# A mixture-of-experts decoder step: four weight units of the last job fetched before the expert loop

## The chip, the cores and the metric

The kernel runs on one core of a Trainium2 chip. The metric is the device time of one execution in microseconds (us); lower is better. The engines are named as in the profile: PE (TensorE, matrix products; PEld is its weight load), DVE (VectorE), ACT (ScalarE), POOL (GpSimd) and SP (SyncE, which here only starts transfers). Sixteen DMA engines move the data; SP, ACT and POOL each have a queue of their own into them.

## The reference

One decoder layer on 512 prompt rows and 8 sample rows of width 1024. A mixer (pooling, dilated attention, gated convolution) and an output projection come first, then a layer norm, then a mixture of experts:

```python
logits = einsum('md,de->me', xt, router_w) + router_b      # 520 rows, 32 experts
top_v, top_i = top_k(logits, 4);  gates = softmax(top_v)
hh = xblk @ e_w_in[e] + e_b_in[e]                           # 1024 -> 2048
gate, up = split(hh, 2);  gate = min(gate, 7);  up = clip(up, -7, 7)
act = gate * sigmoid(1.702 * gate) * (up + 1)
y += gate_weight * (act @ e_w_out[e] + e_b_out[e])          # 1024 -> 1024
x = layer_norm(alpha * x + y)
```

Everything is in 32-bit floats. An expert has 8 MB of input weights and 4 MB of output weights, and all 32 experts are used, so the expert weights are some 400 MB.

## The kernel before

There are two program blocks, one after the other, with a barrier of all engines between them.

**The front** (`first_block`) does the mixer, the projection, the first layer norm, the router, and the lists of rows for each expert. It keeps the attention's mix in `mix` (`[P, 8, 520]`) and queries, keys, values and bias rows in `qkv` (`[P, 6*520+2048]`). While it ends, SP fetches the first expert's twelve units into `ring` (L270): three at L565 and later, four after the last attention product, five after the last output projection (`wo3`). POOL splits the output biases into `drow` (L650, L653), which reads `qkv`, and then scatters the row lists to memory (L629). When all lists are there (`listed`), SP reads back six pieces of them (L585, L587) and ACT two (L816). At the same time DVE works out the job table (L1441 to L1502): which expert each job has, and how many groups of 32 rows. So the job order is known only at the end of the front.

**The expert loop** (`moe_block`) runs over jobs, 32 here, one for each expert. The order is by row count through the table `ORDER`; the last job has the expert with the fewest rows. A job has 1 to 5 groups of 32 rows. Its weights are twelve **units** of 1 MB: 8 input units (`ring[0..7]`) and 4 output units (`ring[8..11]`). The ring holds one job's worth, so a unit's slot is loaded anew as soon as PE has used it. The steps of PE for job u are:

- `up`: a bias product (L1747), then for each of 8 input units a wait for it, and the products of each group (L1753; eight PE records for a unit and group);
- `down` of the job before: bias (L1772, L1778), then for each of 4 output units a wait and the products (L1767; sixteen records for a unit and group).

SP, in its loop (around L1621), waits for `up_done` of each input unit of job u and loads that of job u+1, then waits for `down_done` of each output unit of job u-1 and loads that of job u. All weights go through its one queue, in this order: in(u+1) 0 to 7, out(u) 0 to 3, in(u+2) 0 to 7, and so on. DVE turns PE's results into the next operand (`xgT`, `hid`), ACT does the sigmoid and scales the results (L1821), POOL gathers rows (L1667) and adds results into memory (L1676). After the last job the sums are read into `fin` (`[P, 5, 1024]`, a buffer of its own) and the second layer norm ends the program.

PE's groups are a nest of branches, written so that a job with few groups jumps over the code of the others in each unit:

```python
def each_group(groups, f, j=0):
    if j + 1 < JG:
        with pe.If(groups > j + 1):
            each_group(groups, f, j + 1)
    return f(j)
```

Of the kernel before, what the change touches and what calls it, by code (L numbers as in the profile page):

```python
# [29 lines left out]
P = 128  # L30
D = 1024
KT = D // P
SEQ = 512
NS = 8
R = SEQ + NS
HALF = R // 2
NT = SEQ // P
# [18 lines left out]
GS = 32  # L56
# [9 lines left out]
NWORD = -(-(MAXJ + 1) // 3)  # L66
AHEAD = 6
UNITS = 12
LAST_TILES = (4, 0, 1, 2, 3)
PAD0 = R + 4  # L70
ORDER = (0, 30, 10, 9, 15, 11, 22, 1, 25, 21, 24, 7, 18, 5, 17, 14, 23, 2, 28, 19, 4, 16, 12, 26, 8, 20, 3, 27, 6, 29, 13, 31)
# [162 lines left out]
def layer(nc, xT, x_prompt, x_sample, pool_prefix, conv_prefix, state_pool, state_conv, cache_k, cache_v,  # L234
          w_in, pool_w, chan, w_o, ln1_g, ln1_b, router_w, router_b, e_in, e_brow, e_out, e_bout,
          ln2_g, ln2_b, consts, lists0, pbias,
          y_prompt, y_sample, p_pool, p_conv, p_k, p_v, s_pool, s_conv, s_k, s_v):
    x1_dram = nc.dram_tensor("x1_rows", [R, D], F32).ap()
    acc_dram = nc.dram_tensor("acc_rows", [R, D], F32).ap()
    q_dram = nc.dram_tensor("sample_queries", [NS, ATTW], F32).ap()  # L240
    lists_dram = nc.dram_tensor("list_rows", [GS, NE * MAXQ, 2], F32).ap()

    with ExitStack() as outer:
        def keep(name, shape, dt=F32):
            return outer.enter_context(nc.sbuf_tensor(name, shape, dt))

        def sem(name):
            return outer.enter_context(nc.semaphore(name))


        ring = keep("ring", [P, UNITS, 2048])
        cst = keep("cst", [P, NCONST])
        lists = keep("lists", [P, NE * MAXQ, 2])
        brow = keep("brow", [P, NQ, 2, QC], BF16)
        drow = keep("drow", [P, D], BF16)
        jobs = keep("jobs", [1, 6, NJT], I32)
        count = keep("job_count", [1, 1], I32)

        def C(name, rows=P):
            lo, hi = CONST[name]  # L260
            return cst[0:rows, lo:hi]

        unit_in = [sem(f"unit_in{u}") for u in range(UNITS)]
        lists_in = sem("lists_in")
        more_lists_in = sem("more_lists_in")

        def load_unit(eng, e, j):

            src = e_in[bass.ds(e, 1), j] if j < KT else e_out[bass.ds(e, 1), j - KT]
            eng.dma_start(ring[:, j], src.rearrange("o p n -> p (o n)")).then_inc(unit_in[j], 16)  # L270

        first_block(nc, locals())
        moe_block(nc, locals())
# [3 lines left out]
def first_block(nc, o):  # L277

    xT, x_prompt, x_sample, w_in, w_o, cache_k, cache_v, state_pool, state_conv = (
        o[k] for k in "xT x_prompt x_sample w_in w_o cache_k cache_v state_pool state_conv".split())  # L280
    ring, lists, lists_in, more_lists_in, jobs, count, brow, drow, C, load_unit = (
        o[k] for k in "ring lists lists_in more_lists_in jobs count brow drow C load_unit".split())
    x1_dram, acc_dram, lists_dram, q_dram = o["x1_dram"], o["acc_dram"], o["lists_dram"], o["q_dram"]


# [29 lines left out]
    with ExitStack() as ctx:  # L315
        def sb(name, shape, dt=F32):
            return ctx.enter_context(nc.sbuf_tensor(name, shape, dt))

        def bsem(name):
            return ctx.enter_context(nc.semaphore(name))  # L320
# [2 lines left out]
        late = xt[:, :, :].rearrange("p k r -> p (k r)")  # L323
        l1g, l1b = late[:, 0:D], late[:, D:2 * D]
        x1t = late[:, 2 * D:4 * D].rearrange("p (u k r) -> p u k r", u=2, k=KT)
        mix = sb("mix", [P, KT, R])
        scr = mix[:, 2:4, :]
        scr2 = mix[:, 4:6, :]
        prod = mix[:, 2:4, :].rearrange("p a r -> p (a r)")[:, 0:2 * ATTW].rearrange("p (t f) -> p t f", t=2)
        up = sb("up", [P, 2, PBUF + R])  # L330
        qkv = sb("qkv", [P, 6 * R + 2 * FF])
        qT = qkv[:, 0:3 * R].rearrange("p (i r) -> p i r", i=3)
        kT = qkv[:, 3 * R:6 * R].rearrange("p (i r) -> p i r", i=3)
        v = qkv[:, 6 * R:6 * R + (NT + 1) * ATTW].rearrange("p (i f) -> p i f", f=ATTW)
# [121 lines left out]
        counted = bsem("counted")  # L456
        ranks_read = bsem("ranks_read")
        split = bsem("bias_split_steps")
        brow_ready = bsem("brow_ready")
        placed_in_lists = bsem("placed_in_lists")  # L460
        listed = bsem("listed")
# [30 lines left out]
        def _(sp):  # L492
# [87 lines left out]
            sp.wait_ge(stored, 16 * (NT + 1 + 4))  # L580
            sp.wait_ge(copied, 48)
            sp.wait_ge(k_stored[1], 32)
            sp.wait_ge(listed, 16 * TOPK * (NT + 1))
            for c in (0, 2):
                sp.dma_start(lists[c * GS:(c + 1) * GS, 0:NE * JG], lists_dram[:, 0:NE * JG]).then_inc(lists_in, 16)  # L585
            for c in range(NQ):
                sp.dma_start(lists[c * GS:(c + 1) * GS, NE * JG:], lists_dram[:, NE * JG:]).then_inc(more_lists_in, 16)  # L587

        @block.gpsimd
        def _(gp):  # L590
# [67 lines left out]
                keep_high_out(part * NE, (part + 1) * NE)  # L658
            take_off_out(2 * NE, 3 * NE)
            keep_high_out(2 * NE, 3 * NE)  # L660
            for i in range(NT):
                list_rows(i, i + 2)

        @block.scalar
        def _(a):
# [146 lines left out]
                x1_store(i, i + 2)  # L812
                top_exps(i, i + 2)
            a.wait_ge(listed, 16 * TOPK * (NT + 1))
            for c in (1, 3):
                a.dma_start(lists[c * GS:(c + 1) * GS, 0:NE * JG], lists_dram[:, 0:NE * JG]).then_inc(lists_in, 16)  # L816
            a.wait_ge(x1_sent, 32 * (NT + 1))

        @block.tensor
# [708 lines left out]

def moe_block(nc, o):

    ring, lists, lists_in, more_lists_in, brow, drow, jobs, count, C, sem, load_unit, unit_in = (
        o[k] for k in "ring lists lists_in more_lists_in brow drow jobs count C sem load_unit unit_in".split())
    x1_dram, acc_dram = o["x1_dram"], o["acc_dram"]
    x1_quarters = x1_dram.rearrange("r (c n) -> (r c) n", n=QC)
    acc_quarters = acc_dram.rearrange("r (c n) -> (r c) n", n=QC)
# [1 line left out]
    with ExitStack() as ctx:  # L1537
# [16 lines left out]
        gate4 = sb("gate4", [P, AHEAD, JG])  # L1554
        l2g = sb("l2g", [P, D])
        l2b = sb("l2b", [P, D])
        fin = sb("fin", [P, NT + 1, D])
        zeros = sb("zeros", [P, 1], BF16)
        bn2 = sb("bn2", [P, 2, 2, 6])
        mv2 = sb("mv2", [P, NT + 1, 5])  # L1560
# [49 lines left out]
        def _(sp):  # L1610
# [10 lines left out]
            with sp.Fori(1, MAXJ) as u:  # L1621
                with sp.If(u + 1 < last):
                    e = expert_of(u + 1)
                    for k in range(KT):
                        sp.wait_ge(up_done, KT * u + k + 1)
                        load_unit(sp, e, k)
                with sp.Else():
                    sp.nop()
                with sp.If(u < last):
                    e = expert_of(u)  # L1630
                    for q in range(FT // 2):
                        sp.wait_ge(down_done, FT // 2 * u + q + 1)
                        load_unit(sp, e, KT + q)
                with sp.Else():
                    sp.nop()
# [96 lines left out]
        def _(pe):  # L1732
# [10 lines left out]
            def up(groups, step):  # L1743

                def bias(j):
                    for c in range(NQ):
                        nc.tensor.matmul(pu[quarter(c), j], chosen[:, :], brow[:, c],  # L1747
                                         start=True, stop=False, skip_group_check=True)

                def unit(k, j):  # L1750
                    w = ring[:, k].rearrange("p (a n) -> p a n", a=2)
                    for c in range(NQ):
                        mm = nc.tensor.matmul(pu[quarter(c), j], xgT[:, j, k], w[:, :, c * QC:(c + 1) * QC],  # L1753
                                              start=False, stop=k == KT - 1, skip_group_check=True)
                    return mm
                each_group(groups, bias)
                for k in range(KT):
                    pe.wait_ge(unit_in[k], 16 * step)
                    each_group(groups, lambda j: unit(k, j)).then_inc(up_done, 1)

# [261 lines left out]
```

## Time and profile before

| | |
|---|---|
| median of 3 runs | 1390.07 us (1389.95 to 1390.19) |
| the profiled execution's own time | 1392.93 us |
| its span, first to last instruction | 1390.8 us |
| mean granted TensorE clock | 0.948 of full |
| PE busy | 1210.8 us (87%) |
| DVE busy | 509.2 us (37%) |
| moved by DMA | 463.13 MB |
| share of the DMA engines, SP's queue | 77.8% |

The span is some 2 us shorter than the execution's own time, and that execution took 2.86 us more than the median of the runs. Busy time of PE is from modelled ends of pipelined matmuls. In the rows, "x8" is a count of instructions, and the brackets give idle time before them with what ended it.

### The profile page before, as it was taken

What the parts mean: (1) busy time and instruction counts of PE and PEld (TensorE: products, weight loads), DVE (VectorE), ACT (ScalarE), POOL (GpSimd) and SP (SyncE); (2) the same over time, 40 slices, a digit from 0 to 9 for tenths busy, and PEclk for the clock granted to TensorE, in tenths of its full rate; (3) what the DMA queues carried; (4) which work ended last, traced back from release to release, by engine and by line L of the source; (5) the groups of instructions that cost most, each with busy time, mean ns of one, the idle gap of its engine ahead of it and who ended that gap; (6) DMA issues with size and microseconds to landing.
All of it is one profiled execution on the core that took longest, in us unless ns stands there. A gap on an engine that the chain in (4) does not pass through costs nothing.

```text
span 1390.8 us, 33184 instructions
## 1 busy us (share of the span) xinstructions
PE 1210.8 (87%) x12380; PEld 539.8 (39%) x12381; DVE 509.2 (37%) x825; ACT 177.6 (13%) x351; POOL 314.5 (23%) x263
## 2 busy tenths in 40 slices
PE   6998989883789999999979998998998989996880
PEld 5886434361233333344333433362342323432230
DVE  1997624275422222224231332132222231414226
ACT  0013222220010000001000010010000010101103
POOL 7000112624121232013212132124121212130113
PEclk9999999975899999999999999999999999998975
DMA  9601840281999999999999999999999999999973
GB/s 342 193 3 61 263 163 3 95 311 53 410 415 417 409 406 400 416 409 394 414 416 407 414 404 414 392 414 397 416 409 405 408 416 407 381 401 419 408 292 125
DMA packets 86538, 463.13 MB, mean 333 GB/s; under 512 B 13508, under 2 KB 29609, under 8 KB 36205
## 3 DMA queue, kind: packets, MB, share of 16 engines
q1 hardware_dynamic: 67915, 438.55, 77.8%
q0 software_dynamic: 16528, 17.88, 5.9%
q10 hardware_dynamic: 2066, 6.32, 1.2%
q8 instruction: 17, 0.28, 0.1%
q14 instruction: 12, 0.10, 0.0%
HBM read 448.29 MB, written 19.48 MB: 336 GB/s over the span
## 4 chain that ended last, share of the span: by engine, by line
PE 51%; DMA 19%; issue 3%; DVE 2%; SPq 1%; ACT 0%; DVEq 0%; ACTq 0%; POOLq 0%
PE pu L1753 32%; PE rest L1767 17%; DMA ring<-in_e_in 12%; DMA ring<-in_e_out 6%; PE pu L1747 1%; PE rest L1778 1%; SPq L270 1%; DVE fin L1954 0%; DVE bn L1936 0%; DVE mv L1947 0%; DMA acc_rows<-y,idx 0%; PE rest L1772 0%; DMA fin<-acc_rows 0%; DVE xgT L1875 0%; ACT y L1821 0%
## 5 line engine op out<-in xcount | busy, mean ns | idle before, releaser
L1753 PE MATMUL pu<-ring,xgT 128*32 128x512 f32 x5248 | 592.1, 604 | 36.6 <-DMA ring<-in_e_in 34.9
L1753 PEld LDWEIGHTS pu<-ring,xgT 128*32 128x32 f32 x5248 | 164.2, 111 | 445.8 <-issue 443.2
L1767 PE MATMUL rest<-ring,hid 128*32 128x256 f32 x5248 | 299.6, 384 | 18.4 <-DMA ring<-in_e_out 12.5
L1676 POOL DMA_INDIRECT acc_rows<-y,idx x82 | 130.4, 1591 | 763.2 <-ACT y L1821 734.3
L1905 DVE TENSOR_SCALAR gg<-pu 128x1280 f32<-128x1280 f32 x32 | 47.7, 1492 | 613.1 <-PE pu L1753 604.6
L1767 PEld LDWEIGHTS rest<-ring,hid 128*32 128x32 f32 x5248 | 177.4, 111 | 130.9 <-issue 35.0
L1813 ACT ACTIVATE ss<-gg 128x1280 f32<-128x1280 f32 x32 | 40.7, 1273 | 670.6 <-DVE gg L1905 670.6
L836 PE MATMUL pair<-xt,ring 128*128 128x260 f32 x448 | 101.1, 389 | 12.3 <-DMA ring<-in_w_in 12.3
L1667 POOL DMA_INDIRECT xq<-x_rows,idx x82 | 86.1, 1050 | 57.2 <-issue 44.8
L836 PEld LDWEIGHTS pair<-xt,ring 128*128 128x128 f32 x448 | 86.6, 194 | 25.7 <-DMA ring<-in_w_in 12.0
L1821 ACT ACTIVATE y<-rest,gate 128x256 f32 x160 | 61.9, 479 | 252.6 <-PE rest L1767 252.6
L1162 DVE SCALAR_TENSOR_TENSOR conv<-conv,chan_sb 128x512 f32<-128x512 f32 x90 | 70.2, 779 | 3.1
L1747 PE MATMUL pu<-brow,chosen 128*32 128x512 bf16 x328 | 25.1, 403 | 42.9 <-issue 30.1
L1875 DVE STREAM_TRANSPOSE xgT<-xq 128x1280 f32<-128x1280 f32 x33 | 49.7, 1505 | 0.0
L1922 DVE STREAM_TRANSPOSE hid<-uu 128x1280 f32<-128x1280 f32 x32 | 48.2, 1505 | 0.0
L1917 DVE TENSOR_TENSOR uu<-uu,ss 128x1280 f32<-128x1280 f32 x32 | 47.7, 1492 | 1.1
L1915 DVE SCALAR_TENSOR_TENSOR uu<-uu,gg 128x1280 f32<-128x1280 f32 x32 | 47.5, 1484 | 0.0
L1907 DVE TENSOR_SCALAR uu<-pu 128x1280 f32<-128x1280 f32 x32 | 47.4, 1481 | 0.0
L641 POOL TENSOR_SCALAR ring<-ring,negm 128x128 f32<-128x128 f32 (+3 forms) x24 | 26.9, 1125 | 87.6 <-DVE negm L1404 87.5
L1920 DVE CAST chosen_down<-cst 128x32 bf16 x32 | 5.8, 182 | 107.2 <-PE rest L1767 104.1
L968 PE MATMUL pair<-ring,mix 128*128 128x512 f32 x80 | 35.8, 594 | 0.0
L1747 PEld LDWEIGHTS pu<-brow,chosen 128*32 128x32 bf16 x328 | 6.5, 97 | 61.9 <-issue 59.6
(264 smaller groups left out, 613.4 us busy)
## 6 DMA issues: line engine op xcount, KB each, us to landing
ring<-in_e_in SPq DMA_DIRECT2D x256, 1024.0 KB
ring<-in_e_out SPq DMA_DIRECT2D x128, 1024.0 KB
ring<-in_w_in SPq DMA_DIRECT2D x3, 1536.0 KB, 24.0
ring<-in_w_in SPq DMA_DIRECT2D x6, 512.0 KB, 12.4
xt<-in_xT SPq DMA_DIRECT2D x2, 1040.0 KB, 11.0
ring<-in_w_o SPq DMA_DIRECT2D x1, 2048.0 KB, 12.0
conv<-in_x_prompt SPq DMA_DIRECT2D x1, 2048.0 KB, 13.7
x_rows<-conv ACTq DMA_DIRECT2D x4, 512.0 KB
```

The source lines that it names most:

```text
L836: mm = nc.tensor.matmul(b[:, h, 0:HALF], wtile[:, tiles_of(lo, lo + P).start, k], xt[:, k, h * HALF:(h + 1) * HALF], start=k == 0, stop=k ...
L1162: ch.mark(V.scalar_tensor_tensor(cy[:, i, 0:SEQ], u[:, i, t:t + SEQ], taps[:, i, t:t + 1], cy[:, i, 0:SEQ], ALU.mult, ALU.add))
L1667: nc.gpsimd.indirect_dma_start(out=xq[:, u % 2, j], out_offset=None, in_=x1_quarters, in_offset=bass.IndirectOffsetOnAxis(ap=idx4[:, u % A ...
L1676: nc.gpsimd.indirect_dma_start(out=acc_quarters, out_offset=bass.IndirectOffsetOnAxis(ap=idx4[:, u % AHEAD, j:j + 1], axis=0), in_=y[:, u ...
L1753: mm = nc.tensor.matmul(pu[quarter(c), j], xgT[:, j, k], w[:, :, c * QC:(c + 1) * QC], start=False, stop=k == KT - 1, skip_group_check=True)
L1767: mm = nc.tensor.matmul(py[quarter(c), j], hid[:, j, 2 * q + f], w[:, f, c * QC:(c + 1) * QC], start=False, stop=q == FT // 2 - 1 and f == ...
L1821: ins = nc.scalar.activation(y[:, bass.ds(u % 2, 1), j].rearrange("p o n -> p (o n)"), py[:, j], ACT.Copy, scale=ring4[:, bass.ds((u % AHE ...
L1875: V.transpose(xgT[:, :, :, :].rearrange("p j k s -> p (j k s)"), xq[:, half].rearrange("p j n -> p (j n)")).then_inc(turned, 1)
L1905: V.tensor_scalar(gg[:, :, :], pu[:, :, 0], SW_LIMIT, None, ALU.min).then_inc(g_ready, 1)
L1915: at.do(V.scalar_tensor_tensor(uu[:, :, :], uu[:, :, :], 1.0, gg[:, :, :], ALU.add, ALU.mult))
L1917: V.tensor_tensor(uu[:, :, :], uu[:, :, :], ss[:, :, :], ALU.mult).then_inc(h_ready, 1)
L1922: V.transpose(hid[:, :, :, :].rearrange("p j f s -> p (j f s)"), uu[:, :, :].rearrange("p j n -> p (j n)")).then_inc(hid_ready, 1)
```

## The change

A constant `KEPT = 4` and one more buffer, `shared`, that lives through both blocks. In the front, `mix` and `qkv` are now views of it; at the end, `fin` is. Between the two uses its first four units' worth, `last_up`, holds input units 0 to 3 of expert index 31, fetched in the front. SP does this right after expert 0's last five units, once POOL has ended the split of the output biases (`drow_ready`). SP no longer waits for the lists; ACT issues all eight list loads. In the loop SP leaves out units 0 to 3 for the last job, and PE reads them from `last_up` there.

```diff
+        shared = keep("shared", [P, KT * R + 6 * R + 2 * FF])
+        last_up = shared[:, 0:KEPT * 2048].rearrange("p (k n) -> p k n", n=2048)
...
+        def load_last_up(eng, k):
+            eng.dma_start(last_up[:, k], e_in[NE - 1, k]).then_inc(last_up_in, 16)
...
-        mix = sb("mix", [P, KT, R])
+        mix = shared[:, 0:KT * R].rearrange("p (k r) -> p k r", r=R)
...
-        qkv = sb("qkv", [P, 6 * R + 2 * FF])
+        qkv = shared[:, KT * R:]
...
             sp.wait_ge(k_stored[1], 32)
-            sp.wait_ge(listed, 16 * TOPK * (NT + 1))
-            for c in (0, 2):
-                sp.dma_start(lists[c * GS:(c + 1) * GS, 0:NE * JG], lists_dram[:, 0:NE * JG]).then_inc(lists_in, 16)
-            for c in range(NQ):
-                sp.dma_start(lists[c * GS:(c + 1) * GS, NE * JG:], lists_dram[:, NE * JG:]).then_inc(more_lists_in, 16)
+            sp.wait_ge(drow_ready, 1)
+            for k in range(KEPT):
+                load_last_up(sp, k)
...
             keep_high_out(2 * NE, 3 * NE)
+            gp.sem_inc(drow_ready, 1)
...
             a.wait_ge(listed, 16 * TOPK * (NT + 1))
-            for c in (1, 3):
+            for c in range(NQ):
                 a.dma_start(lists[c * GS:(c + 1) * GS, 0:NE * JG], lists_dram[:, 0:NE * JG]).then_inc(lists_in, 16)
+            for c in range(NQ):
+                a.dma_start(lists[c * GS:(c + 1) * GS, NE * JG:], lists_dram[:, NE * JG:]).then_inc(more_lists_in, 16)
...
-        fin = sb("fin", [P, NT + 1, D])
+        fin = shared[:, 0:(NT + 1) * D].rearrange("p (i n) -> p i n", n=D)
...
                     e = expert_of(u + 1)
-                    for k in range(KT):
+                    with sp.If(u + 2 < last):
+                        for k in range(KEPT):
+                            sp.wait_ge(up_done, KT * u + k + 1)
+                            load_unit(sp, e, k)
+                    with sp.Else():
+                        sp.nop()
+                    for k in range(KEPT, KT):
                         sp.wait_ge(up_done, KT * u + k + 1)
                         load_unit(sp, e, k)
...
-                for k in range(KT):
+                with pe.If(step < last):
+                    for k in range(KEPT):
+                        pe.wait_ge(unit_in[k], 16 * step)
+                        each_group(groups, lambda j: unit(k, j)).then_inc(up_done, 1)
+                with pe.Else():
+                    pe.wait_ge(last_up_in, 16 * KEPT)
+                    for k in range(KEPT):
+                        each_group(groups, lambda j: unit(k, j, last_up)).then_inc(up_done, 1)
+                for k in range(KEPT, KT):
                     pe.wait_ge(unit_in[k], 16 * step)
                     each_group(groups, lambda j: unit(k, j)).then_inc(up_done, 1)
```

## Rows read from the trace of the kernel before

**Rows 1.** The page's chain that ended last, shares of the span by line.
```profile
PE pu L1753 32%; PE rest L1767 17%; DMA ring<-in_e_in 12%; DMA ring<-in_e_out 6%; PE pu L1747 1%; PE rest L1778 1%; SPq L270 1%; DVE fin L1954 0%; DVE bn L1936 0%; DVE mv L1947 0%; DMA acc_rows<-y,idx 0%; PE rest L1772 0%; DMA fin<-acc_rows 0%; DVE xgT L1875 0%; ACT y L1821 0%
```

**Rows 2.** Windows 385:655 and 655:1335: busy time of each engine, granted clock, DMA share, GB/s.
```profile
385.00:655.00 270.00, 261.57 (x3222) 104.22 (x3222) 74.05 (x82) 27.60 (x53) 63.52 (x48) 1.00 1.03 408
655.00:1335.00 680.00, 612.12 (x7412) 232.89 (x7407) 190.20 (x210) 67.37 (x126) 136.71 (x103) 0.98 1.02 407
```

**Rows 3.** Waits of PE, 385 to 655: us in total, times, longest.
```profile
PE pu L1747 <- issue: 8.3, 9, 1.7
```

**Rows 4.** Waits of PE, 655 to 1336.
```profile
PE pu L1753 <- DMA ring<-in_e_in: 34.6, 36, 1.9
PE rest L1767 <- DMA ring<-in_e_out: 12.5, 14, 2.1
```

**Rows 5.** Timeline of PE at the end: start us, us, what, count, idle before.
```profile
1313.43 1.07 PE L1767 MATMUL rest<-ring,hid 128*32 128x256 f32 x16 [1.41 <-DMA ring<-in_e_out]
...
1315.93 1.07 PE L1753 MATMUL pu<-ring,xgT 128*32 128x512 f32 x8 [0.23 <-issue]
1318.40 1.07 PE L1753 MATMUL pu<-ring,xgT 128*32 128x512 f32 x8 [1.41 <-DMA ring<-in_e_in]
...
1333.88 1.94 PE L1753 MATMUL pu<-ring,xgT 128*32 128x512 f32 x8 [0.54 <-DMA ring<-in_e_in]
...
1336.63 11.21 PE L1767 MATMUL rest<-ring,hid 128*32 128x256 f32 x192
...
1351.29 5.61 PE L1767 MATMUL rest<-ring,hid 128*32 128x256 f32 x64
```

**Rows 6.** Timeline of SP's queue at the end: in(31), then out(30) and out(31).
```profile
1290.32 18.35 SPq L270 DMA_DIRECT2D ring<-in_e_in  x8
1309.84 38.55 SPq L270 DMA_DIRECT2D ring<-in_e_out  x8
```

**Rows 7.** Windows 1332:1334 and 1336:1338, columns as in rows 2.
```profile
1332.00:1334.00 2.00, 1.46 (x12) 0.12 (x8) 0.00 (x0) 0.00 (x0) 0.00 (x0) 0.50 0.57 242
1336.00:1338.00 2.00, 2.00 (x28) 0.90 (x32) 2.00 (x2) 0.59 (x1) 0.00 (x0) 0.50 0.23 98
```

**Rows 8.** Timeline of POOL in the front: last step of the bias split, last list scatter.
```profile
268.83 1.03 POOL L650 CAST drow<-qkv 32x1024 bf16<-32x1024 f32 x1
...
321.92 0.98 POOL L629 DMA_INDIRECT list_rows<-pairs,spots  x1 [0.30 <-issue]
```

**Rows 9.** Timeline of SP's queue in the front.
```profile
290.62 0.54 SPq L270 DMA_DIRECT2D ring<-in_e_out  x1
...
324.96 1.82 SPq L587 DMA_DIRECT2D lists<-list_rows  x4
```

**Rows 10.** Timeline of ACT in the front: last store of normed rows, list loads.
```profile
308.54 0.45 ACTq L751 DMA_DIRECT2D acc_rows<-conv  x1
...
324.06 0.88 ACTq L816 DMA_DIRECT2D lists<-list_rows  x2
```

**Rows 11.** Timeline of DVE around the barrier.
```profile
329.91 0.19 DVE L1502 SCALAR_TENSOR_TENSOR jobs<-xt 1x52 int32<-1x52 f32 x1
331.07 0.17 DVE L1866 COPY gate<-lists 128x5 f32<-128x5 f32 x1 [0.97 <-PEq L315]
...
335.43 0.16 DVE L1866 COPY gate<-lists 128x5 f32 x1
```

**Rows 12.** Windows 290:312 and 312:322 of the front, columns as in rows 2.
```profile
290.00:312.00 22.00, 17.83 (x93) 16.36 (x92) 15.26 (x59) 7.07 (x15) 7.94 (x8) 0.58 1.00 383
312.00:322.00 10.00, 2.34 (x21) 1.81 (x20) 7.74 (x43) 0.39 (x2) 6.94 (x8) 0.50 0.03 5
```

**Rows 13.** Timeline of PE: start and products of a five-group job, then a one-group job.
```profile
540.88 1.26 PE L1747 MATMUL pu<-brow,chosen 128*32 128x512 bf16 x20 [0.49 <-issue]
541.96 34.51 PE L1753 MATMUL pu<-ring,xgT 128*32 128x512 f32 x320
...
907.97 7.08 PE L1753 MATMUL pu<-ring,xgT 128*32 128x512 f32 x64
```

More of the change, by code:

```diff
@@ L68 @@
 UNITS = 12
+KEPT = 4
 LAST_TILES = (4, 0, 1, 2, 3)
@@ L263, in layer @@
         unit_in = [sem(f"unit_in{u}") for u in range(UNITS)]
+        last_up_in = sem("last_up_in")
         lists_in = sem("lists_in")
@@ L280, in first_block @@
         o[k] for k in "xT x_prompt x_sample w_in w_o cache_k cache_v state_pool state_conv".split())
-    ring, lists, lists_in, more_lists_in, jobs, count, brow, drow, C, load_unit = (
-        o[k] for k in "ring lists lists_in more_lists_in jobs count brow drow C load_unit".split())
+    ring, shared, lists, lists_in, more_lists_in, jobs, count, brow, drow, C, load_unit, load_last_up = (
+        o[k] for k in "ring shared lists lists_in more_lists_in jobs count brow drow C load_unit load_last_up".split())
     x1_dram, acc_dram, lists_dram, q_dram = o["x1_dram"], o["acc_dram"], o["lists_dram"], o["q_dram"]
@@ L458, in first_block @@
         split = bsem("bias_split_steps")
+        drow_ready = bsem("drow_ready")
         brow_ready = bsem("brow_ready")
@@ L1529, in moe_block @@
 def moe_block(nc, o):
-    ring, lists, lists_in, more_lists_in, brow, drow, jobs, count, C, sem, load_unit, unit_in = (
-        o[k] for k in "ring lists lists_in more_lists_in brow drow jobs count C sem load_unit unit_in".split())
+    ring, shared, last_up, lists, lists_in, more_lists_in, brow, drow, jobs, count, C, sem, load_unit, unit_in, last_up_in = (
+        o[k] for k in ("ring shared last_up lists lists_in more_lists_in brow drow jobs count C sem load_unit unit_in "
+                       "last_up_in").split())
     x1_dram, acc_dram = o["x1_dram"], o["acc_dram"]
@@ L1748, in bias, with unit @@
                                          start=True, stop=False, skip_group_check=True)
-                def unit(k, j):
-                    w = ring[:, k].rearrange("p (a n) -> p a n", a=2)
+                def unit(k, j, of=ring):
+                    w = of[:, k].rearrange("p (a n) -> p a n", a=2)
                     for c in range(NQ):
```

## The prediction

> **What bounds the kernel now.** I read the chain that ended last, then the windows, then PE's waits, and last the timelines of PE and of SP's queue at the end. In the chain the reader is to see that PE's two products and the transfers of the two kinds of weights share the span, 49% to 18% [rows 1]. That alone does not say which of the two sets the end. The windows do: from 385 to 1335 us the DMA engines are busy throughout (share 1.03 and 1.02, at 408 and 407 GB/s), while PE is busy 261.57 of 270 and 612.12 of 680 us [rows 2]. Up to 655 PE waits for no transfer at all, only some 0.9 us at the start of each of nine steps [rows 3]. After 655 it waits for weights 50 times, 47.1 us in all [rows 4]. So the stream of weights has no gap and sets the time; PE works close behind it and absorbs what it can in those 50 waits. A byte that leaves this stream should shorten the span, if PE does not become the limit where it leaves, and if the byte's new place is free.
>
> **What the change takes out at the end.** The last job has one group, so PE does a unit of it in 1.07 us at full clock, and it stands waiting for the next: its units 1 and 7 start at 1318.40 and 1333.88 [rows 5], which is 15.48 / 6 = 2.58 us a unit. The queue order behind that is in(31) 0 to 7, out(30) 0 to 3, then out(31) 0 to 3 [rows 6]. The change leaves out in(31) 0 to 3, so everything behind in the queue comes 4 x 2.58 = 10.3 us earlier. The queue does not run dry through this: out(29) 3 lands just before 1313.43 [rows 5], and in(31) 4 to 7 are issued when up(30) frees their slots, by 1308.3 (the end of 18.35 us from 1290.32, less the last issue) [rows 6].
>
> Then PE's side, step by step, because the whole 10.3 us counts only if PE follows:
>
> - up(31) starts at 1315.9 as before. Units 0 to 3 lie ready: 4 x 1.07 = 4.3 us, to 1320.2. Unit 4 is in by then; unit 7 comes at 1333.88 - 10.3 = 1323.6 and its product ends at 1324.7.
> - down(30), three groups, began at 1336.63 and took 11.21 us [rows 5]. If out(30) follows in(31) at the same pace, its units are usable at 1326.2, 1328.8, 1331.3 and 1333.9. PE's 11.21 us began at half clock (granted 0.50 until 1338 [rows 7]); at full clock throughout I estimate 10.5, or 2.6 us a unit, the pace of the transfers. So it goes from 1326.2 to 1336.7. Before, it ended at 1347.84. That is 11.1 us.
> - down(31) waits, from the end of down(30), for DVE to turn `hid` and for ACT to empty the sums; that took 1351.29 - 1347.84 = 3.45 us and does not change. So it starts at 1340.2. out(31) is issued as the slots come free, after each unit of down(30), as now. It moves with down(30), and its 5.61 us too.
> - What follows, 1356.9 to 1390.8 = 33.9 us (last scatter, reading the sums, layer norm, stores), is the same work; `fin` has a new address only.
>
> The extra 0.8 us beyond 10.3 is clock and wait. The granted clock was 0.50 at the last units of up(31) [rows 7], each of which took 1.94 instead of 1.07 us [rows 5]; before the fall PE had worked 1.07 of each 2.5 us. With four units at hand PE is busy nearly all the time from 1315.9, and I expect full clock there.
>
> One thing in the rows has to be settled for this sum. The DMA share falls to 0.57 at 1332 to 1334 and to 0.23 at 1336 to 1338 [rows 7], yet down(30) shows no wait. Most engines thus have finished out(30) by 1334, and a few, 0.23 x 16 = 4 or fewer, work on. A unit counts as in only when its last engine is done, so the 2.58 us pace is that of the slowest engines, and I let out(30) land at that pace. If all sixteen were even, out(30) would be in by about 1334 now and 1324 then; down(30) would start right behind up(31), at 1325.2, end at 1335.7, and the gain would be 12.1 us. The Trainium skill ("DMA: Bandwidth & Descriptors", Latency and other measured facts) says that DMA engines 7 and 15 are usually slower than the others in traces; by that rule the first of the two sums, 11.1 us, is the right one, and the window at 1336 agrees in kind, with a share near that of a few engines.
>
> **What it adds in the front.** 4 MB more from SP's queue. SP issues expert 0's last unit at 290.62 [rows 9]; the bias split for which it now waits ended at 269.9 [rows 8], so that wait costs nothing, and nothing is behind it on SP but the barrier. The four issues take about 1.8 us (four list loads took 1.82 [rows 9]). The transfers need 10.3 us. The engines are full from 290 to 312 and nearly idle from 312 to 322 [rows 12], so the traffic ends near 322.5 instead of 312. ACT's last store of normed rows is issued at 308.54 [rows 10] and will land later, but is awaited only after the lists. The lists are what matters: POOL's last scatter is issued at 321.92 to 322.9 [rows 8] and seen as landed at 324.1, when the list loads start [rows 10]. The new traffic has ended about then, on slow engines perhaps 2 us later.
>
> The list loads themselves: ACT issues eight instead of two, 0.44 us each [rows 10], so its last starts 2.6 us later than its second did, at about 327.2, against SP's last now at 326.4 [rows 9]. Nobody needs them yet: DVE writes the job table until 330.1, all engines pass the barrier at 331.0, and DVE reads the first lists at 331.07 and the second part at 335.43 [rows 11]. The slack is some 3 us for ACT to reach the barrier, and 5 us or more for the second part. Bounds: 0 if all lands as said; 3 us if a list scatter is held up behind weights and the barrier moves; below 0 there is nothing, since SP's own list loads were not on the path. I take 0.2.
>
> If the cover of idle engines from 312 to 322 were gone, the fetch would cost its 10.3 us again and the change would be worth nothing but the 0.8.
>
> **What it adds in the loop.** On SP one comparison and a branch a job, before the first load; the queue is far ahead (in(31) unit 0 is issued at 1290.32 and unit 1 used at 1318.40 [rows 5, 6]), so 0. On PE a comparison in each step, and after unit 3 a jump over the new code of the other branch: 4 units x 5 groups x 16 instructions = 320. The trace has no such jump. From below: a one-group job jumps over 64 instructions in each of 8 units, and its 64 products take 7.08 us where the five-group job's pace gives 64 x 34.51 / 320 = 6.90 [rows 13]; that is 0.02 us a jump. From above: the start of a step, with the jump back over the whole body, three waits and several branches, shows 0.49 us [rows 13] and at most 1.7 [rows 3]. By length the new jump is nearer to the first, and I take 0.1 us. Nine steps without a wait for transfers make 0.9 us, behind a stream that has no gap there, and after 655 the 47.1 us of waits take the rest: 0 on the path. With 0.5 us a step the nine steps make 4.5 us, of which I would still expect most hidden.
>
> **The sum.** 11.1 - 0.2 = 10.9 us. The profiled execution took 1392.93 us, span 1390.8, so the same view of the changed kernel should show a span of 1379.9. The median of the runs was 2.86 us under the profiled execution's time; the same difference in time from the median is 1390.07 - 10.9 = **1379.2 us**.
>
> **Rivals.**
>
> 1. *The jump is dear.* The start of a step can cost 1.5 us or so, and the new jump lands 320 instructions on. If it cost 1.5 us, the nine steps to 655 would make PE 13.5 us late where it has no wait to give back; the ring would fill, the stream would stop, and the net would be at worst 1390.07 - 10.9 + 13.5 = 1392.7, slower. It turns from gain to loss at 10.9 / 9 = 1.2 us a step, later if the ring's stock covers a part. For it: 8.3 us in nine starts [rows 3]. Against it: 0.02 us a jump within units [rows 13]. The Trainium skill ("Runtime: NRT & Kernel Launch", Instruction fetch mechanics) says that a taken branch whose target is outside the window of fetched pages stalls until the page is there, and gives the page as 256 instructions; by that rule each of the 31 steps pays a fetch, and no row here shows its length for such a jump. Half price, 0.5 to 1.2 us, gives 1380 to 1390. Chance: 0.05 for slower, 0.08 for a part of the gain lost.
> 2. *The front slips.* Scatters of the lists wait behind 4 MB of weights, and the barrier moves by 1 to 3 us: 1380.5 to 1382.5. For it: the engines are full until 322 and POOL's last scatter is issued at just that time. Against: POOL issued eight of them beside full engines from 301 on (x8 in 290 to 312 [rows 12]), and each is small. Chance 0.13.
> 3. *The clock falls anyway.* PE's busy share before 1315.9 is low in both kernels. At half clock up(31) takes 8 x 1.94 = 15.5 us to 1331.4, and down(30) ends at 1343: the gain is 5, 1385. Chance 0.05.
> 4. *The fetch replaces nothing.* If SP's skip starved the queue, in(31) 4 would be late; it is issued near 1300, 13 us before out(29) 3 lands, so I give this 0.02, at 1388 to 1391.
>
> The forecast itself has 0.67. From these: faster by over 0.2% (2.8 us, about what a measurement of this kernel can tell from no change) 0.91, within 0.2% 0.04, slower 0.05. The range for 8 in 10 takes in the even-engine sum (1378.0 with nothing lost in front) and the slipped front up to 1383.
>
> **What would show it.** In the profile after: the DMA share in 312 to 322 near 1 instead of 0.03; the barrier still near 331; the first 28 jobs at the same times to within 1 us; up(31) without a wait in its first four units and with full clock; down(30) ending near 1336.7; the DMA share falling below 0.6 near 1322; 33.9 us after PE's last product. If the starts of steps are unchanged but a gap of more than 0.5 us stands inside `up` after unit 3, rival 1 is at work. If the whole loop is shifted by a constant from 331 on, rival 2. If the span falls by less than 8 us with neither, the queue order was not what set the end.

## The result: the changed kernel is slower by 31%

The changed kernel took 1824.3 us (1822.5 to 1827.8, four runs), the kernel before 1390.0 us on the same chip (1387.5 to 1390.2, four runs). The ratio is 1.313, 95% interval 1.311 to 1.315. The profiled execution has a span of 1821.6 us against 1390.8, and a mean granted clock of 0.866 against 0.948. Some executions are longer for no reason in the kernel (1442.4 us of e6, 1447.3 and 1458.4 of e11, 2535.5 of e10 in the experiments below), and the ratios leave them out.

The forecast was 1379.2 us, with a range from 1378.0 to 1383. What the change was meant to do does happen at the end, as e4 and e12 show; but PE's loop has grown by one branch, and that makes each of its 31 full steps 13.9 us longer.

The changed kernel leaves one thing out: it fetches the four units of expert 31 and uses them for whichever expert has the last job. On this input that is expert 12 with 10 rows, while expert 31 has 22 rows and an earlier job (e11's expectation gives both counts). So the first four units of the last job are another expert's, and the results of those 10 rows are not the reference's. The same holds for e4, e6, e7, e8, e10 and e12; e11 and e13 put expert 31 last. The number and size of products and transfers are the same either way, so the times can be compared.

### The profile page after: what moved, and what is told of

Same layout as the page of the kernel before. It is cut to its first block, busy times and chain, and to the rows that moved or that the text cites. A ratio compares the mean times of both kernels' runs of the same rounds, so it can differ in the third digit from the quotient of the medians.

```text
span 1821.6 us, 33355 instructions
## 1 busy us (share of the span) xinstructions
PE 1328.5 (73%) x12380; PEld 549.9 (30%) x12381; DVE 508.6 (28%) x825; ACT 177.5 (10%) x351; POOL 313.1 (17%) x263
## 3 DMA queue, kind: packets, MB, share of 16 engines
q8 instruction: 290, 4.75, 1.1%
## 4 chain that ended last, share of the span: by engine, by line
PE 57%; issue 22%; DVE 1%; DMA 0%; ACT 0%; DVEq 0%; ACTq 0%; POOLq 0%
PE pu L1770 36%; PE rest L1792 18%; PE pu L1764 2%; PE rest L1803 1%; DVE shared L1979 0%; DVE bn L1961 0%; PE rest L1797 0%; DVE mv L1972 0%; DMA acc_rows<-y,idx 0%; DVE xgT L1900 0%; ACT y L1846 0%; DMA shared<-acc_rows 0%; DVE idx L1892 0%; ACT shared L1875 0%; DVE shared L1990 0%
## 5 line engine op out<-in xcount | busy, mean ns | idle before, releaser
L1770 PE MATMUL pu<-ring,xgT 128*32 128x512 f32 x5216 | 650.8, 657 | 115.3 <-issue 115.3
L1792 PE MATMUL rest<-ring,hid 128*32 128x256 f32 x5248 | 337.7, 409 | 96.8 <-issue 96.2
L1770 PEld LDWEIGHTS pu<-ring,xgT 128*32 128x32 f32 x5216 | 171.0, 120 | 584.9 <-issue 584.7
L1764 PE MATMUL pu<-brow,chosen 128*32 128x512 bf16 x328 | 41.0, 622 | 192.6 <-issue 181.2
L978 PE MATMUL pair<-ring,shared 128*128 128x512 f32 x80 | 35.8, 594 | 0.0
## 6 DMA issues: line engine op xcount, KB each, us to landing
xt<-in_xT SPq DMA_DIRECT2D x2, 1040.0 KB, 11.1
```

What stands on the lines that cost most here:

```text
L1792: mm = nc.tensor.matmul(py[quarter(c), j], hid[:, j, 2 * q + f], w[:, f, c * QC:(c + 1) * QC], start=False, stop=q == FT // 2 - 1 and f == ...
```

## The profile after

The page of the changed kernel: the chain that ended last by engine, the two product lines (busy us, mean ns of one; idle before them and what ended it), and the queues of weights and of instructions (packets, MB, share of 16 engines).

```profile
q1 hardware_dynamic: 67627, 437.98, 64.0%
...
q8 instruction: 290, 4.75, 1.1%
...
PE 57%; issue 22%; DVE 1%; DMA 0%; ACT 0%; DVEq 0%; ACTq 0%; POOLq 0%
...
L1770 PE MATMUL pu<-ring,xgT 128*32 128x512 f32 x5216 | 650.8, 657 | 115.3 <-issue 115.3
L1792 PE MATMUL rest<-ring,hid 128*32 128x256 f32 x5248 | 337.7, 409 | 96.8 <-issue 96.2
```

The same queues on the page of the kernel before:

```profile
q1 hardware_dynamic: 67915, 438.55, 77.8%
...
q8 instruction: 17, 0.28, 0.1%
```

The transfers of weights, 18% of the chain before [rows 1], are gone from it, and "issue" stands in their place: PE waited for nothing that the profile follows. The one row that says what it waited for is q8, the queue that brings instructions: 290 packets in place of 17.

PE's waits in the changed kernel from 340 us on (us in total, times, longest), which answer to [rows 3, 4]:

```profile
PE pu L1764 <- issue: 181.2, 31, 7.7
PE pu L1770 <- issue: 120.2, 44, 4.9
PE rest L1792 <- issue: 96.2, 55, 4.4
```

and in the kernel before, from 340 to 1352 us:

```profile
PE pu L1753 <- DMA ring<-in_e_in: 34.9, 37, 1.9
PE pu L1747 <- issue: 30.1, 29, 5.7
PE rest L1767 <- DMA ring<-in_e_out: 12.5, 14, 2.1
PE rest L1767 <- issue: 5.0, 5, 3.2
...
PE pu L1753 <- issue: 1.4, 5, 0.4
```

The reader sees three things. The waits for "issue" add up to 397.6 us against 36.5. They stand at the start of every step (31 times, 5.8 us each on average) and also inside `up` and `down`, where no semaphore is waited for. And PE no longer waits for weights at all. The bill of the 430.8 us: waits for issue +361 on these lines and +5 on two others, waits for weights -47, waits for DVE and ACT -4, PE busy 1328.5 us in place of 1210.8, which is +118 (with the same products at a lower clock); together 433.

The timeline of PE in the changed kernel (start, us, what, count, idle before) shows where the pauses are:

```profile
396.28 1.47 PE L1764 MATMUL pu<-brow,chosen 128*32 128x512 bf16 x12 [5.37 <-issue]
397.53 12.07 PE L1770 MATMUL pu<-ring,xgT 128*32 128x512 f32 x96
412.31 10.57 PE L1770 MATMUL pu<-ring,xgT 128*32 128x512 f32 x96 [2.71 <-issue]
422.81 0.23 PE L1797 MATMUL rest<-zeros,brow 128*128 128x1 bf16 x3
422.97 0.29 PE L1803 MATMUL rest<-drow,chosen_down 128*32 128x256 bf16 x4
423.09 1.47 PE L1792 MATMUL rest<-ring,hid 128*32 128x256 f32 x24
427.43 2.23 PE L1792 MATMUL rest<-ring,hid 128*32 128x256 f32 x24 [2.87 <-issue]
432.82 1.93 PE L1792 MATMUL rest<-ring,hid 128*32 128x256 f32 x16 [3.15 <-issue]
442.40 1.47 PE L1764 MATMUL pu<-brow,chosen 128*32 128x512 bf16 x12 [7.65 <-issue]
```

One of these pauses lies after 96 products of a three-group `up`: that is the jump over the new branch, and it costs 2.71 us here. But `down` is the same code as before and pauses twice, and the start of the step pauses 5.4 to 7.7 us. So it is not the new jump alone that is dear; the whole loop is fetched again in every step.

Windows of the changed kernel, columns as in [rows 2]:

```profile
312.00:322.00 10.00, 1.99 (x19) 1.46 (x18) 7.88 (x47) 0.39 (x2) 6.88 (x8) 0.50 0.95 384
340.00:1750.00 1410.00, 1015.60 (x10890) 355.98 (x10882) 280.77 (x310) 97.44 (x181) 206.28 (x157) 0.86 0.80 286
```

The first is the new fetch in the front (DMA share 0.95 against 0.03 [rows 12]). In the second the DMA share is 0.80, against 1.02 and more [rows 2]: the stream of weights waits for PE and no longer sets the time.

## The theory

The instructions of PE come in pieces of 16 KB: a packet of q8 is 4.75 MB / 290 = 16.4 KB, and at the 64 bytes that an instruction has in the compiled program that is 256. I counted the loop in the compiled program for PE. Before, it has 1449 instructions; after, 1788, because the other branch of `up` holds four units for up to five groups once more. The pauses inside steps with known group counts lie at instructions 256 apart, which gives the borders of the pieces. The places below (9.38 and so on) count in such pieces from the start of PE's program; the lengths are counted, while the borders are inferred from the pauses and can be wrong by a few instructions. By them the loop runs from 9.38 to 15.04 pieces before, and touches seven (9 to 15). After, it ends at 16.37 and touches eight. My theory: a loop that touches seven pieces stays in the engine and is fetched once; one that touches eight is fetched anew in each pass, 273 packets more over 31 steps, 8.8 a step. From 340 us to the end the kernel before fetched 8 packets in all.

The rival is the one of the prediction: taken jumps are dear by themselves, and the new ones cost what is lost. Others are the new fetch in the front, and the change's own new wait and buffer.

One more thing about the loop is needed below. It is two loops, one inside the other: the outer one reads a word with the sizes of three jobs, the inner one does three steps. In the compiled program the outer loop adds only seven instructions, five ahead of the inner one and two behind it.

## Experiments

Where a kernel ran once, a single time stands; a ratio with an interval comes from several runs of both kernels. On different chips the median of the kernel before lay between 1389.0 and 1393.9 us, and its single runs up to 1401.7.

### Code that is never executed (e1, e2, e3)

The kernel before, with n dead units (code of a unit that no step executes) between units 3 and 4 of `up`, n = 4, 3, 2 in e1, e2, e3 (the loop over the units is written in two parts around them):

```diff
+                with pe.If(step > last):
+                    for k in range(n):
+                        each_group(groups, lambda j: unit(k, j)).then_inc(up_done, 1)
```

> The kernel before, with its weights, order and buffers, plus four units' worth of products for up to five groups (337 instructions) behind a branch in PE's loop that is never taken. Theory A (PE's loop no longer fits what PE keeps of its program, so every step fetches all of it anew): about 1820 to 1850 us, and some 8 to 9 instruction-queue packets of 16 KB a step, like the changed kernel's 290 in all. Theory B (the early fetch, the skipped loads or the wait on the new buffer are to blame): 1390 us and 17 packets. Theory C (each taken jump over long code costs a fetch, whatever the loop's size): slower than 1390, with about one fetch a step, some 50 packets in all.

> As the kernel with four dead units, with three (253 instructions more than before). Theory A with pieces of 256 instructions at fixed places: the loop now ends about 8 instructions into an eighth piece, so it should be as slow as with four, over 1700 us. If size alone mattered smoothly, three quarters of the loss, about 1710 us or less. Theory C: near the kernel before plus one fetch a step. Theory B: 1390 us.

> As the kernel with four dead units, with two (169 instructions more than before); the loop lies in seven pieces of 256, as in the kernel before. Theory A: 1390 us to within 3, 17 packets on the instruction queue. Smooth in size: about 1600 us. Theory C: as with three and four dead units.

Measured: 1817.14 us with four units (loop of 1786 instructions, to 16.36 pieces), 1809.5 us with three (1702, to 16.03), 1392.99 us with two (1618, to 15.70); the kernel before on the same chip took 1390.37. The waits of PE in e1 from 340 us on:

```profile
PE pu L1747 <- issue: 177.7, 30, 8.3
PE pu L1753 <- issue: 117.5, 43, 4.3
PE rest L1773 <- issue: 91.7, 55, 4.4
```

and q8 of e2, then of e3:

```profile
q8 instruction: 290, 4.75, 1.2%
```

```profile
q8 instruction: 17, 0.28, 0.1%
```

So the loss comes out whole without the change: no fetch in the front, no other buffer, no new semaphore, only code in the loop that nothing executes. e1 shows the pauses of the changed kernel, each of the three sums within 5 us. It is a cliff and no slope. e2 reaches 8 instructions into the eighth piece and costs as much as e1 with 92; 84 instructions fewer cost nothing that one run can tell (2.6 us). All three have the same kind of taken jump (over some 168 to 336 instructions), which speaks against the jump by itself; e5 below settles it, with e2's own jump.

### The same code at another place (e5, e7, e6)

Instructions that are never executed, this time ahead of the loop; they make it no longer and only move it against the borders (n is 90 in e5, 79 in e6, 50 in e7; a product is two instructions, and the comparison one more):

```diff
             last = job_count(pe)
+            with pe.If(last > NJT - 10):
+                for _ in range(n):
+                    nc.tensor.matmul(rest[:, 0, 0:1], brow[:, 0, 0, 0:P], zeros[:, :],
+                                     start=True, stop=True, skip_group_check=True)
```

e5 is e2 moved by 181 instructions (to 10.09 to 16.74: seven pieces). e6 is the changed kernel moved by 159 (10.00 to 16.99: seven, with 1 and 3 instructions to spare). e7 is the changed kernel moved by 101 (9.78 to 16.76: eight still).

> The kernel with three dead units, instruction for instruction, with 181 more instructions ahead of PE's loop that a branch jumps over. The loop has the same length but now starts 23 instructions into a piece of 256 and so lies in seven pieces instead of eight. Theory A with fixed pieces: 1390 to 1393 us and 17 packets on the instruction queue, where the unmoved one had 1809 us and 290. Theory A' (the length of the loop decides, wherever it lies): about 1810 us. Theory C (long jumps): about 1810 us.

> The changed kernel with 101 instructions ahead of the loop instead of 159: the same kind of edit, but the loop still touches eight pieces. Theory A: as slow as the changed kernel, about 1820 us, 290 packets. If putting any code there is what helps: near 1379 us.

> The changed kernel as it is, with 159 instructions ahead of PE's loop that a branch jumps over, so that its 1788 instructions fall into seven pieces of 256 (start 1 to 2 instructions into the first, end 3 before the end of the seventh, if I read the places right). Theory A: 1376 to 1382 us, best 1379. If the place is off by three instructions: over 1800 us. Theory B: 1824 us.

Measured: e5 1388.25 us with 18 packets on q8, where e2 took 1809.5 with 290. The two loops are instruction for instruction the same, jumps included. This decides it: what counts is how many pieces the loop touches, not how long it is, and a jump over some 250 instructions in every step costs no fetch. e7 gave 1842.01 us and 283 packets, no better than the change itself: code ahead of the loop is no cure by itself. e6 gave 1428.8 us (1415.9 to 1442.4, six runs; ratio 1.024, 1.020 to 1.028), nearly 400 us less than the change but not the time expected. Its page and PE's timeline:

```profile
q8 instruction: 55, 0.90, 0.2%
```

```profile
718.73 7.08 PE L1792 MATMUL rest<-ring,hid 128*32 128x256 f32 x128
739.12 1.04 PE L1764 MATMUL pu<-brow,chosen 128*32 128x512 bf16 x8 [13.31 <-issue]
739.95 8.75 PE L1770 MATMUL pu<-ring,xgT 128*32 128x512 f32 x64
756.32 4.38 PE L1770 MATMUL pu<-ring,xgT 128*32 128x512 f32 x20 [7.62 <-issue]
```

Some steps still fetch. Which ones, the timeline says. These are the starts of steps 4 to 7:

```profile
414.14 1.47 PE L1764 MATMUL pu<-brow,chosen 128*32 128x512 bf16 x12 [7.60 <-issue]
...
449.73 0.83 PE L1764 MATMUL pu<-brow,chosen 128*32 128x512 bf16 x12 [0.58 <-issue]
...
483.04 0.83 PE L1764 MATMUL pu<-brow,chosen 128*32 128x512 bf16 x12 [0.52 <-issue]
...
523.10 1.04 PE L1764 MATMUL pu<-brow,chosen 128*32 128x512 bf16 x8 [7.26 <-issue]
```

It goes on so to the end: steps 4, 7, 10 and so on to 31 start after a pause of 7.2 to 13.3 us, and no other step from the third on after more than 1.7; e11 has the same pattern. Those are the passes of the outer loop. So the inner loop stays, and the fetch comes only when the few instructions of the outer one are executed. That fits an error of a few instructions in my borders, by which the outer loop alone reaches into an eighth piece; a border error that put the inner loop over it too would have given the whole loss, as the expectation says and e2 shows. e13 gives more room.

### The change without the growth (e4, e12)

The other branch does the one group that the last job has here, and no more; it leaves the code for two to five groups out:

```diff
                     for k in range(KEPT):
-                        each_group(groups, lambda j: unit(k, j, last_up)).then_inc(up_done, 1)
+                        unit(k, 0, last_up).then_inc(up_done, 1)
```

The loop has 1516 instructions and ends at 15.30: seven pieces, with the comparison, the jump, the front and the buffer as in the change.

> The changed kernel, but its branch for the last job has the products of one group instead of up to five (the last job has one group here), so the loop is 272 instructions shorter and lies in seven pieces. Everything else of the change is there. Theory A: the forecast effect comes out, 1376 to 1382 us, with the fetched units used and up(31) without waits in its first four units. Theory B: about 1820 us still. Theory C: the jump is still there but short; between.

> The changed kernel with one group in its other branch, as in e4, timed in rounds now. Its loop on PE has 1516 instructions and touches seven pieces of 256. Theory (the loop must stay within seven pieces): 1379 to 1381 us in the median, ratio to the kernel before 0.992 to 0.994, and 17 packets of instructions in the profile. Rival (the one look of e4 was lucky, and the change is worth what e8 and e10 showed, 5 us): 1383 to 1386 us.

Measured: e4 1379.72 us, span 1377.6. e12, in several runs, 1385.76 us against 1393.86 of the kernel before beside it; ratio 0.9934 (0.9910 to 0.9957), a gain of 9.2 us (6.0 to 12.5). The ratio is the theory's, while the time in us lies in the rival's range, because the kernel before took 3.8 us more there than the 1390.1 us from which the theory's was reckoned. Both have 17 packets on q8. The end of e12 on PE, which answers to [rows 5]:

```profile
1316.18 5.34 PE L1770 MATMUL pu<-shared,xgT 128*32 128x512 f32 x32
1321.33 3.88 PE L1770 MATMUL pu<-ring,xgT 128*32 128x512 f32 x32
...
1327.41 10.81 PE L1792 MATMUL rest<-ring,hid 128*32 128x256 f32 x192 [1.17 <-DMA ring<-in_e_out]
...
1341.63 2.80 PE L1792 MATMUL rest<-ring,hid 128*32 128x256 f32 x48
1344.72 1.07 PE L1792 MATMUL rest<-ring,hid 128*32 128x256 f32 x16 [0.29 <-DMA ring<-in_e_out]
```

Spans of single executions are to be compared from the barrier on, because the time up to it differs from one to the next. It shows as DVE's first read of the lists, in the kernel before at 331.07 [rows 11], in e9 and e12 here:

```profile
325.76 0.17 DVE L1884 COPY gate<-lists 128x5 f32<-128x5 f32 x1 [0.97 <-PEq L323]
```

```profile
331.60 0.17 DVE L1891 COPY gate<-lists 128x5 f32<-128x5 f32 x1 [0.97 <-PEq L323]
```

From there to the end of the span the kernel before takes 1390.8 - 331.1 = 1059.7 us, e12 1380.5 - 331.6 = 1048.9, e4 1049.3 (its barrier is at 328.3). So the gain in the profile is 10.8 and 10.4 us; the prediction had 11.1 for it. How far such a figure scatters is seen on profiles with the work and the transfers of the kernel before and a loop that is held: 1058.2 us in e3, 1059.0 in e5, 1059.7 in the kernel before, 1059.9 in e9.

### The front alone, and fewer units (e9, e8, e10)

e9 fetches the four units in the front and doesn't use them: PE's loop, shown here, and SP's, and with them the order of transfers, are those of the kernel before.

```diff
-                with pe.If(step < last):
-                    for k in range(KEPT):
-                        pe.wait_ge(unit_in[k], 16 * step)
-                        each_group(groups, lambda j: unit(k, j)).then_inc(up_done, 1)
-                with pe.Else():
...
+                for k in range(KEPT):
+                    pe.wait_ge(unit_in[k], 16 * step)
+                    each_group(groups, lambda j: unit(k, j)).then_inc(up_done, 1)
```

e8 is the change with `KEPT = 2` (1620 instructions, to 15.71), e10 with `KEPT = 3`, moved by 181 as e5 was (1704 instructions, 10.09 to 16.75); both touch seven pieces.

> The front of the change alone: the four units are fetched into the shared buffer and the list loads are ACT's, but the loop loads and uses all twelve units of the last job from the ring, as before. What the front costs stands alone. I forecast 0.2 us, bounds 0 to 3: 1390.2 us (1390 to 1393).

> The change with KEPT = 2: two units fetched early and two in the doubled branch, loop of 1620 instructions in seven pieces. Theory A, and 2.58 us for each unit taken out of the stream: 1390.0 - 5.2 + 0.2 = 1385 us (1383.5 to 1386.5), 17 packets. Theory C (each long jump costs a fetch): over 1400 us. Theory B: about halfway to the changed kernel's time, 1600 us.

> KEPT = 3 with 181 instructions ahead of the loop, seven pieces. Theory A with 2.58 us a unit: 1390.0 - 7.7 + 0.2 = 1382.5 us (1381 to 1384). If PE's side decides at the end (up(31) and down(30) back to back), the third and fourth unit bring less and this lies within 1 us of the version with four.

Measured: e9 ratio 0.9993 (0.9978 to 1.0009), so the front costs nothing that can be measured (bound: 1.3 us). e8 1384.12 us, ratio 0.9961 (0.9946 to 0.9977), e10 1383.72 us, ratio 0.9949 (0.9930 to 0.9967), with 17 and 18 packets on q8. From the barrier to the end the profiles give 1059.9 us for e9, 1055.7 for e8, 1052.6 for e10, and 1048.9 and 1049.3 for the four units of e12 and e4: 4.0, 7.1 and 10.6 us less than before, 2.0 to 2.7 us a unit. The gain grows with the units, as the pace of 2.58 us a unit said.

### Towards a version that does all groups (e11, e13)

e11 is e6 with a table of ties in which expert 31 always comes last:

```diff
-    tie = np.where(np.arange(NE) == 0, 1e6, -np.arange(NE))
+    tie = np.where(np.arange(NE) == 0, 1e6, np.where(np.arange(NE) == NE - 1, -1e6, -np.arange(NE)))
```

e13 has this too (expert 31 comes last whatever its count, more than its expectation says), is moved by 165, and does the four units of a group in a row, so that one nest of comparisons is enough:

```diff
-                    for k in range(KEPT):
-                        each_group(groups, lambda j: unit(k, j, last_up)).then_inc(up_done, 1)
+                    each_group(groups, lambda j: [unit(k, j, last_up) for k in range(KEPT)][-1]).then_inc(up_done, KEPT)
```

> The changed kernel with the loop moved into seven pieces, and the table that orders the experts gives expert 31 the last job, so that the units fetched early are the last job's own (its 22 rows are one group, as the 10 of expert 12, and the group counts of all jobs stay). 1379 us, within 0.5 us of the moved kernel without that.

> The changed kernel with all five groups in its other branch, but one nest of comparisons there in place of four (each group does its four units in a row): the loop on PE has 1776 instructions in place of 1788. 165 instructions that are never executed stand ahead of it, so that it starts 7 instructions behind a border of 256 and ends 9 before one; among experts with equally few groups number 31 is put last. e6 had the same loop with 1 and 3 instructions to spare. Theory A (only instructions that are executed count): seven pieces, 17 or 18 packets of instructions, no gap inside up, 1379 to 1382 us. Theory B (the engine fetches some way ahead of what it executes, so that nearness to the border is enough for an eighth piece): 30 to 60 packets of instructions and 1400 to 1440 us, as in e6.

Measured: e11 1441.7 us in the median of six runs (1425.3 to 1458.4; ratio 1.033, 1.028 to 1.038) with 55 packets on q8, like e6 and 60 us over its expectation. e13 1387.61 us (1384.1 to 1390.6, eight runs) against 1393.86, ratio 0.9945 (0.9923 to 0.9968), and

```profile
q8 instruction: 16, 0.26, 0.1%
```

With 1776 instructions in seven pieces and 7 and 9 to spare nothing is fetched again; 1 and 3 were too few. This excludes a fetch that reaches far ahead. In e6 the refetch in every third step alone speaks for borders that are off by a few instructions; that the engine looks one or two instructions ahead is not excluded. e13 is the only version here that beats the kernel before and gives the last job its own expert's weights for any number of groups.

Its time is not the 1379 to 1382 us of its expectation. From the barrier (334.5) its profile gains 5.7 us and not 10.8, in part because its clock is low again as `down(30)` begins:

```profile
1332.00:1336.00 4.00, 3.83 (x44) 2.07 (x48) 3.97 (x7) 0.73 (x1) 0.00 (x0) 0.62 0.17 74
```

With the barriers of both profiles laid on each other, the difference from e12 comes in three parts. The third unit of `down(29)` already starts 1.8 us later (1316.38 - 3.47 against 1311.65 - 0.53). `down(30)` takes 12.25 us in place of 10.81, with the clock at 0.62 in its first 4 us. `down(31)` takes 6.41 in place of 4.16, with the clock at 0.57 and 0.60 where e12 has 1.00. Its order of jobs is another; whether that makes the first part, and why the clock falls here and not in e12, is not shown.

## Why the prediction was wrong, point by point

- **What bounds the kernel now:** right. The stream sets the end, and each unit taken out of it gives 2.0 to 2.7 us (e8, e10, e12).
- **The end:** right in mechanism and nearly in size. Set on the barrier of the kernel before, `down(30)` was to start at 1326.2 and end at 1336.7. In e12 it starts at 1327.41 - 0.53 = 1326.9, after a wait for its weights as said, and ends at 1337.7. The sum was 11.1 and is 10.4 to 10.8. The full clock came only from 1320 on: the four units that lay ready took 5.34 us in place of 4.3 in e12, and 3.64 in e4. The first of the two sums for out(30) was the right one: the wait of 1.17 us before `down(30)` shows that its first unit is not in when most engines fall idle. In e12 the DMA share is 0.25 from 1326 to 1328, the share of four engines of sixteen. By the Trainium skill's remark on two slower engines ("DMA: Bandwidth & Descriptors", Latency and other measured facts) it was to be so; no run here shows which engines they are.
- **The front:** 0.2 us, bounds 0 and 3; e9 has -1.0 (-3.1 to 1.3). Right. The barrier was to stay near 331; in six profiles with the new fetch (e4, e8, e9, e10, e12, e13) it lies between 325.8 and 334.5, and in five without it (the kernel before, e1, e2, e3, e5) between 327.1 and 332.7, so a single profile could not have told a shift of 2 us.
- **The loop:** this is the step that failed. The prediction has a jump over 320 instructions, "0.1 us a step" and "0 on the path", bounded by 0.02 and 1.7 us. The jump is not what costs. The term left out is the code itself: 339 more instructions in a loop of 1449 take it from seven pieces to eight. Measured: (1821.6 - 1390.8) / 31 = 13.9 us a step, eight times the upper bound, and in `down` and at the step's start as much as at the jump. The bound was taken from jumps inside a loop that was in the engine as a whole; no row of such a loop can price one that is not. The row to read was q8: 17 packets of 256 instructions in a program of which 1449 are passed 32 times. It said that the loop was held, and thus that there was a room that it could outgrow.
- **Rival 1** came nearest and had the gaps at the right line, with 0.13 of the chance in both its parts. Its price of at most 1392.7 was 432 us too low, for the same reason. Its turning point, 1.2 us a step, was passed by 12.7 us.
- **The Trainium skill** ("Runtime: NRT & Kernel Launch", Instruction fetch mechanics) gives 128 KiB of instruction memory for PE and blocks of 16 KiB. That is eight blocks; here seven stay and eight do not (e2, e3, e5). The prediction used of that section the sentence on taken branches and the page of 256 instructions, but not the size of the memory, against which the loop's 1449 and 1788 instructions could have been held. The stall at each taken branch that the prediction drew from it for rival 1 does not show where the loop is held: e5 makes such a jump in every step and has 18 packets in all. By the size alone both would have seemed to fit in 2048; by the runs, the borders and the eighth block decide.
- **Rivals 2 to 4** did not occur, but for the clock at the very beginning of up(31).

## What to carry to other kernels

When a change puts code into a loop of an engine, count the engine's instructions from the loop's first to its last, those of branches that are never taken too, and ask how many pieces of 256 the loop touches where it lies. Of nested loops count the outer one, and leave some instructions of room at both ends (7 and 9 were enough here, 1 and 3 were not). Seven stayed on TensorE here and eight cost 13.9 us a pass, some 1.6 us for each piece fetched. The packets of the instruction queue tell at a glance: few more than the program's length means the loop is held, and a count that grows with the passes is a cliff that no other term of the sum can outweigh. A second copy of a loop's body for one special pass should be as small as that pass allows.

## What the runs showed of the hardware

- The kernel with a loop of 1702 instructions on TensorE took 1388.25 us or 1809.5 us by the loop's place alone (e5, e2). Here 181 instructions ahead of the loop, jumped over once, made the difference.
- Where only the outer of two nested loops seems to reach into an eighth piece, the refetch comes once in a pass of the outer one: pauses of 7.2 to 13.3 us in every third step, 55 packets and 1428.8 us in place of 290 and 1824.3 (e6).
- Each step of the changed kernel fetched 8.8 pieces, more than the eight it touches, and (1821.6 - 1390.8 + 10.6) / 273 = 1.6 us of span went with each. Why it is more than eight is not shown.
- With the pauses the clock is lower as well: 0.86 in 340 to 1750 us against 1.00 and 0.98 [rows 2], and PE's own busy time is 118 us longer, more than a quarter of the loss. The pair with the same loop shows it too: 0.88 and 0.87 in e2 against 1.00 and 0.97 in e5, from 385 to 655 and from 655 to 1335 us.
